# Routing tables by expert on 32 partitions, rows without empty ones, modulation units inside the router

## The reference, cut to what matters

```python
g_idx = argmax(h @ grp_w + grp_b)                 # one group of 4
top_v, top_i = top_k(e_logit_of_that_group, 2)    # two of its 8 experts
w = g_prob * softmax(top_v)
out[token] += w * ((silu(x @ w_gate[e]) * (x @ w_up[e])) @ w_down[e])   # for both experts e
x = x + g2 * out
```

## Time and profile before

| | |
|---|---|
| three runs | 3595.5 us median (3585.95 to 3603.7) |
| the profiled execution | 3583.24 us, its span 3581.4 us |
| PE / VectorE / ScalarE / POOL busy | 86% / 34% / 21% / 13% |
| granted PE clock, mean | 0.919 |
| chain that ended last, by engine | PE 66%, DMA 18%, VectorE 10% |
| of it waiting for expert weights | 16% |
| read from and written to DRAM | 616.92 MB, 42.99 MB |

### The profile page before, as it was taken

How to read it: one execution, slowest core, us unless ns; L and a number is a source line. 1 busy time by engine, 2 the same in 40 slices (tenths; PEclk the granted TensorE clock), 3 DMA queues, 4 the chain that set the end, 5 groups by cost and what they waited for, 6 DMA issues and landing times.

```text
span 3581.4 us, 36439 instructions
## 1 busy us (share of the span) xinstructions
PE 3069.8 (86%) x15346; PEld 2112.8 (59%) x15346; DVE 1235.5 (34%) x2375; ACT 744.8 (21%) x1331; POOL 472.5 (13%) x477
## 2 busy tenths in 40 slices
PE   5979598888849889869888865999998888899997
PEld 3757555444437655355454425888646677488875
DVE  4984500000035533230000005323273875332334
ACT  3233111000022143201000003212111233222222
POOL 0130122221110033012222210000001321000000
PEclk9989699999978999979999987999998898999998
DMA  6572499999851231259999963222212002122221
GB/s 243 194 181 97 157 358 398 411 397 396 332 203 60 71 122 67 120 184 396 402 394 400 385 257 117 94 94 94 77 60 97 1 1 83 36 94 99 89 86 50
DMA packets 138697, 662.37 MB, mean 185 GB/s; under 512 B 9504, under 2 KB 81568, under 8 KB 104608
## 3 DMA queue, kind: packets, MB, share of 16 engines
q0 software_dynamic: 40560, 428.89, 31.3%
q1 hardware_dynamic: 96816, 226.09, 17.7%
q10 hardware_dynamic: 1152, 4.98, 0.4%
HBM read 616.92 MB, written 42.99 MB: 184 GB/s over the span
## 4 chain that ended last, share of the span: by engine, by line
PE 66%; DMA 18%; DVE 10%; ACT 2%; issue 2%; POOL 1%; POOLq 1%; DVEq 0%; SPq 0%; ACTq 0%
PE ps L87 64%; DMA ring<-in_exp_up,wix 16%; DVE scr L101 3%; PE ps L90 2%; DVE scr L109 1%; ACT hT L93 1%; DVE hT L109 1%; DVE scr L115 1%; DVE scr L121 1%; DVE hT_r L101 1%; DVE scr L112 1%; POOLq L134 1%; DVE ring_r L101 1%; ACT scr L93 1%; POOL ring L130 1%
## 5 line engine op out<-in xcount | busy, mean ns | idle before, releaser
L87 PE MATMUL ps<-ring,scr 128*64 128x512 f32 (+3 forms) x3136 | 757.8, 577 | 115.5 <-DMA ring<-in_exp_up,wix 114.1
L87 PE MATMUL ps<-ring_r 128*128 128x512 f32 (+1 forms) x2544 | 754.1, 378 | 37.2 <-DVE hT_r L101 36.6
L87 PEld LDWEIGHTS ps<-ring,scr 128*64 128x64 f32 (+2 forms) x3136 | 305.1, 160 | 482.5 <-issue 472.2
L87 PEld LDWEIGHTS ps<-ring_r 128*128 128x128 f32 x2544 | 471.8, 192 | 149.5 <-issue 47.2
L87 PE MATMUL ps<-scr,ring 128*128 128x128 f32 (+2 forms) x3744 | 481.9, 292 | 56.2 <-DMA ring<-yrows,nix 30.9
L87 PEld LDWEIGHTS ps<-scr,ring 128*128 128x128 f32 x3744 | 450.6, 200 | 85.2 <-issue 34.8
L87 PE MATMUL ps<-hT_r,ring_r 128*128 128x512 f32 (+1 forms) x1224 | 462.8, 378 | 0.0
L101 DVE TENSOR_TENSOR scr<-scr,ps 64x512 f32<-64x512 f32 (+1 forms) x72 | 49.7, 691 | 844.8 <-ACT scr L93 525.7
L87 PE MATMUL ps<-scr_r,ring_r 128*128 128x512 f32 x1104 | 259.6, 395 | 0.6 <-DVE scr_r L101 0.6
L87 PEld LDWEIGHTS ps<-hT_r,ring_r 128*128 128x128 f32 x1224 | 236.2, 193 | 40.1 <-issue 1.8
L87 PE MATMUL ps<-ring 128*128 128x512 f32 (+9 forms) x712 | 201.8, 520 | 47.4 <-ACT ring L97 24.9
(11 more groups left out here) (143 smaller groups left out, 2548.7 us busy)
## 6 DMA issues: line engine op xcount, KB each, us to landing
ring<-in_ffn_w SPq DMA_DIRECT2D x66, 1024.0 KB, 5.3
ring<-in_mod_w SPq DMA_DIRECT2D x16, 2048.0 KB, 7.7
ring<-in_mod_w SPq DMA_DIRECT2D x16, 1024.0 KB, 4.9
yrows<-scr SPq DMA_DIRECT2D x88, 128.0 KB, 9.3
yrows<-scr SPq DMA_DIRECT2D x20, 512.0 KB, 11.2
ring<-in_exp_gate SPq DMA_DIRECT2D x4, 2048.0 KB, 14.8
ring<-in_exp_up SPq DMA_DIRECT2D x4, 2048.0 KB, 19.2
ring<-in_exp_down SPq DMA_DIRECT2D x4, 2048.0 KB, 23.6
```

The lines of the kernel that those rows point to most:

```text
L87: return self.real.matmul(o, l, r, start=start, stop=stop) if self.real else Quiet()
```

## The change

- **Counts and tables by expert.** The router's weights are padded to 64 columns, and even and odd kt use different halves of the PE columns; the two halves are summed in the matmul that turns the logits (`half_sum`). The counts come out with experts on 32 partitions; rank, place, capacity and overflow of each expert are then one column, and one matmul (`r_p`) spreads 160 columns of results over all partitions. The ranks of the tokens are one bank (`r_k`). One-hot matrices are built in four instructions in all. Work that only the combine needs (`w1`, `w2`, `ox`) stands at the end.
- **Rows.** `rt` holds token numbers above the bound for empty slots, and the gather has `bounds_check`, which leaves those rows out. `yrows` has 1536 rows, one per token and choice, and POOL scatters each block's results straight to them (`pool_outputs`), again without the empty slots. The combine reads them with plain loads on SP. The zero writes are gone.
- **Ends.** No stage end stands between blocks and branch; only POOL reports (`"further"`) to SP.
- **Modulation.** The four units of layer 0's mixture are loaded in halves into scratch and multiplied between the router's steps.
- **Splits.** The first two parts of "at" and "ffn1" are made by ScalarE in the combine and by POOL (`POOL_LOWER`).

```diff
-        for b in range(32):
-            hst = M.hst[:, (b % 2) * 1024:(b % 2) * 1024 + 1024]
-            e.wait_ge(*ps.emptied("e_d", l, b, 0))
...
-                    e.dma(yrows[128 * b:128 * b + 64, 512 * q:512 * q + 512], hst[64 * q:64 * q + 64, 0:512]).then_inc(
-                        *y_out[b % 2].up(l, b, by=16))
-        if l == 0:
-            e.wait_ge(*yg_in[512].of(0))
-            for u in M.mod.units:
-                weights_load(e, 3 + u % 3, ("mod", 1, u), I["mod_w"][1, u], 8, 512)
+        e.wait_ge(*y_out[0].of(l, 30))
+        e.wait_ge(*y_out[1].of(l, 31))
+        e.wait_ge(*pool_step.of("further", l))
+        for a, n in chunks(M.T):
+            for i in tiles_of(a, n):
+                for q in range(2):
+                    r = 768 * q + 128 * i
+                    e.dma(moe_y(l, i, q), yrows[r:r + 128, :]).then_inc(*y_in[a].up(l, i, q, by=16))
...
+        mod_load(0)
+        fixed(0, 0)
+        mod_load(1)
+        fixed(0, 1)
+        mod_load(2)
+        fixed(0, 2)
+        mod_load(3)
+        fixed(1, 0, 1, 2)
...
+    def pool_outputs(e, l, b, *signal):
+        M = moes[l]
+        y = M.hst[:, (b % 2) * 1024:(b % 2) * 1024 + 1024]
+        e.wait_ge(*ps.emptied("e_d", l, b, 0))
+        if wide(b):
+            e.wait_ge(*ps.emptied("e_d", l, b, 1))
+            e.scatter(yrows, M.rw[:, b:b + 1], y, bounds_check=1535, oob_is_err=False).then_inc(*signal)
+        else:
+            e.scatter(yrows.rearrange("r (h c) -> (r h) c", h=2), M.rn[:, b:b + 1], y[:, 0:512], bounds_check=3071,
+                      oob_is_err=False).then_inc(*signal)
...
         for b in range(32):
             if b + 3 < 32:
                 fetch_x(b + 3)
             fetch(b + 2, 0, 1)
             if b >= 1:
                 fetch(b + 1, 2)
-        e.wait_ge(*y_out[0].of(l, 30))
-        e.wait_ge(*y_out[1].of(l, 31))
+                store(b - 1)
+        store(31)
...
-        T3 = M.xr[0].rearrange("p (a b) -> p a b", a=32)
-        go(e.tt(T3, row(M.key), col(M.key), ALU.is_ge))
-        go(e.reduce(M.rank, T3, ADD))
+        go(e.ts(cmp, key, kc, ALU.is_ge))
+        go(e.reduce(rank, cmp, ADD))
...
         pool_blocks(e, l)
-        stage_end(e, f"ov{l}", "act", "dve", "pe")
-        e.wait_ge(*dve_step.of(l, "ox"))
-        e.overflow(nix[0:1, 40:41], lambda: pool_further(e, l), *own_signals)
+        e.drain()
+        e.overflow(nix[0:1, 16:17], lambda: pool_further(e, l), *own_signals)
+        e.drain().then_inc(*pool_step.up("further", l))
...
-        for b in range(47):
-            if b not in WIDE:
-                a = 64 if b < 32 else 0
-                e.dma(yrows[128 * b + a:128 * b + 128, :].rearrange("p (k c) -> p k c", c=128), zero[a:128]).then_inc(
```

More of the change, by code:

```diff
@@ L965, in rows @@
                 m.then_inc(*ps.fill("r_h", l, i, q))
-        for i in range(NT // 2):
-            rows(i)
+        if l == 0:
+            pe_mod_pieces(e, 1)
+        rows(0)
+        rows(1)
         e.wait_ge(*dve_step.of(l, "aa"))
-        for i in range(NT):
-            o = ps.take("r_k", l, i)
-            e.wait_ge(*ps.ready("r_k", l, i))
-            for j in range(i):
-                e.matmul(o[:, 0:32], k("ones"), M.AA[:, j, :], j == 0, False)
-            e.matmul(o[:, 0:32], k("tri"), M.AA[:, i, :], i == 0, True).then_inc(*ps.fill("r_k", l, i))
@@ L975, in pe_router @@
         o = ps.take("r_n", l)
         e.wait_ge(*ps.ready("r_n", l))
-        for j in range(NT):
-            m = e.matmul(o[:, 0:32], k("ones"), M.AA[:, j, :], j == 0, j == NT - 1)
-        m.then_inc(*ps.fill("r_n", l))
-        for i in range(NT // 2, NT):
-            rows(i)
+        e.matmul(o[0:32, 0:32 * NT], k("ones")[:, 0:32], M.AA, True, True).then_inc(*ps.fill("r_n", l))
+        o = ps.take("r_k", l)
+        e.wait_ge(*ps.ready("r_k", l))
+        for s in range(1, NT):
+            e.matmul(o[:, 32 * s:32 * NT], k("ones"), M.AA[:, 0:32 * (NT - s)], s == 1, False)
@@ new lines, in pe_router @@
+        e.matmul(o[:, 32:32 * NT], k("tri"), M.AA[:, 32:32 * NT], False, True)
+        e.matmul(o[:, 0:32], k("tri"), M.AA[:, 0:32], True, True).then_inc(*ps.fill("r_k", l))
+        if l == 0:
+            pe_mod_turn(e, M.mod, 0)
+            pe_mod_pieces(e, 2)
+        o = ps.take("r_p", l)
+        e.wait_ge(*ps.ready("r_p", l))
+        e.wait_ge(*dve_step.of(l, "by_expert"))
+        e.matmul(o[:, 0:160], k("ones")[0:32, :], M.rows[0:32, :], True, True).then_inc(*ps.fill("r_p", l))
+        rows(2)
@@ L990, in act_router @@
+        m.then_inc(*ps.fill("r_r", l))
+        for i in range(4, NT):
+            rows(i)
+        if l == 0:
+            pe_mod_turn(e, M.mod, 2)
+            pe_mod_turn(e, M.mod, 3)
     def act_router(e, l):
@@ new lines, in dve_router @@
+        cnt, key, cmp, kc, rank, place, cap, cc, oc, ov, o6, rows = (p32(x) for x in (
+            M.cnt, M.key, M.cmp, M.kc, M.rank, M.place, M.cap, M.cc, M.oc, M.ov, M.o6, M.rows))
+        e.wait_ge(*ps.filled("r_n", l))
+        e.reduce(cnt, ps.ap("r_n", l)[0:32, 0:32 * NT].rearrange("p (t e) -> p e t", e=32), ADD).then_inc(*ps.empty("r_n", l))
+        e.wait_ge(*ps.emptied("r_n", l))
+        go(e.stt(key, cnt, 32.0, p32(k("krow")), MUL, ADD))
+        go(e.ttr(cmp, key, id32, scale=1.0, scalar=0.0, op0=MUL, op1=ADD, accum_out=kc))
@@ L1916, in pool_attention @@
     def pool_attention(e):
+        for j in range(2):
+            part_lower(e, ("at", j))
         for n in range(32):
```

422 lines of the change are left out of this document (230 added, 192 removed).

## The result

The changed kernel takes 3447.1 us (median of 4 runs, 3444.5 to 3450.2) against 3593.9 before (4 runs, 3586.0 to 3603.7): a ratio of 0.959, 95% interval 0.957 to 0.962, **faster by 147 us**. The forecast was 3499, the range 3463 to 3536: right in sign, outside the range. I account for the 133.

What follows compares the result with a forecast made beforehand. Blocks 9 to 31 were taken as DMA-bound, earlier ones PE-bound, routers bound by small steps. Terms 24 + 24 + 22 + 6 + 18.5 + 2 - 0.3 = 96 off 3583.2 give 3487, 3499 us on the median's footing; range 3463 to 3536.

Steps and rivals of the forecast that it cites:

- 3, rows: Block loops: leaving empty slots out of gather and write in blocks 9 to 31 saves 22 us, bounds 0 and 44.
- rows save in full: Rival for the later blocks: all bytes of empty slots are saved, 44 us, ending at 3477; chance 0.2.
- the engine swizzle: Later blocks: each DMA engine serves eight fixed partitions, engine 0 keeps nearly its whole load, rows save about 8 us.
- rows save nothing: Rival for the later blocks: first partitions' engines keep their load or empty slots still make transfers; 3521, chance 0.2.
- 1, router of layer 0: Layer 0's router: shorter logits, choice, ranks and tables put `rt` 32.5 us earlier; 8.5 given back, 24 us saved.
- 2, router of layer 1: Layer 1's router: the same with four tiles and no modulation, 26 less 2 given back, 24 us saved.
- 4, scatter on POOL: Block loops: 32 scatter issues per layer, about 0.95 us plus 0.3 each, are covered by POOL's wait; cost 0.
- the rival that ends slower: Rival for the block loops: scatters hold up POOL's queue and delay later fetches, 3665 at 9 us each; chance 0.03.
- 5, fetch of y: End of the blocks: scatter, unwaited drain and plain loads save 4 and 8 us; 6 us taken, bounds 12 and -14.
- the rival that charged it: Rival for the blocks' end: the second drain costs as much as the first, 10.10 us, giving 3519; chance 0.1.
- 6, after the combine: Layer 0 after the combine: 25.3 us shrink to 6.8, POOL's splits hidden by the norm; 18.5 us saved.
- 7, splits of ffn1: Layer 1 before ffn1: 4.49 us of VectorE leave the chain, some splitting enters ScalarE; 2 us saved.

Runs made afterwards that it cites:

- gather_all_halves: Changed kernel, but every empty slot gathers row 767 and narrow blocks' x rows come as 2 KB half rows onto all 128 partitions; 3431.0 us.
- before_skip_x: Kernel before, with only the x gathers leaving empty slots out, all y rows still written by SP; 3526.8 us, ratio 0.982.
- late_fixed: Changed kernel, last row tiles ahead of the table matmuls, two modulation units behind, block 1's weights held until the first x gather landed; 3434.0 us.
- splits_dve: Changed kernel, with the subtractions for the attention's and ffn1's first two weights moved from POOL back to VectorE; 3440.9 us.
- gather_all: Changed kernel, but every empty slot gathers row 767, while the scatter still leaves empty slots out; 3509.7 us.

## Why the prediction was right or wrong

- **3, rows: wrong, and the largest part of the miss.** Forecast 22, bounds 0 and 44; it was 69. The step that failed is "At 396 and 395 GB/s that is 18.7 and 25.2 us, 44 in all; that is the upper bound". It took the rate for a property of the chip. The rate was what x rows on half of the partitions left of it (the later blocks run at 395 to 400 GB/s in the kernel before and at 425 to 426 in gather_all_halves, at the same DMA share of 1.01): the gathers alone gave 53, the writes' move to POOL's queue 21 (priced at nothing), and scattered bytes cost nothing in the loops. The rival "rows save in full" had the right direction and the same wrong bound. The 8 us that the engine swizzle led to, and the rival that rows save nothing, are refuted by before_skip_x.
- **1, router of layer 0: half.** Logits (22.7 us from the norm's start, now 19.6) and choice (10.3, now 6.3) saved the 3 and 4 of the forecast. Ranks and tables were to save 26.5 and saved 17.4 (372.66 to 416.4 before, 368.33 to 394.7 now): the step that failed is "So `rt` stands 32.5 earlier, at 384". VectorE was done with the tables at 384.8, but I let the table matmuls start at once, and PE was in a modulation unit that waited for weights until 388.35. Then "the twelve matmuls (1.1)" took 5.3: before, most of them ran beside VectorE's steps, now all twelve follow the last of these. They took 5.3 us at a granted clock of 0.50 (the 1.2 GHz level), and 2.8 in late_fixed at 1.00. The give-back behind it, 8.5 in the forecast, was 10.8 (from `rt` to x 5.1 us before, 15.9 now). In late_fixed `rt` comes at 382.6 and x at 398.4, where the forecast had 384 and 398: the lost time ahead of `rt` is order and clock. The give-back is not: from `rt` to x late_fixed still takes 15.8, since the last row write is issued behind `rt` (384.4) and the gather 9.4 later.
- **2, router of layer 1: right**, 21.8 for 24.
- **4, scatter on POOL: right.** A scatter took 1.01 us on the mean of 64, hidden; the rival that ends slower did not come about.
- **5, fetch of y: wrong by 18.** The step that failed is "drain 10.1 without waiting for the landing": it was 4, which makes 12. The other 6 are a margin: the forecast's own parts gave 4 and 8, and it took 6 in case the drain should grow. The second drain was to cost nothing, rightly; the rival that charged it is out.
- **6, after the combine: right but for one row.** 13.7 for 18.5. "The splits move to POOL, 4.60 each, hidden by the norm (9 us)": the first was not beside the norm but beside VectorE's sums, where a step of 0.41 took 4.24.
- **7, splits of ffn1: wrong sign**, -4 for +2, by the same hold-up; splits_dve gives 3 of each back.
- **The footing.** 12.3 us were added for the median of before; the changed kernel's profile was no such distance below its own, so 15 more went missing. The upper end of the range, 3536, is 3 above what its terms add up to (3499 + 22 + 12).

## What to carry to other kernels

A DMA share of 1.00 says that the engines are busy, not that bytes set the pace (here it stood beside 385 and beside 425 GB/s): look at how long one packet of the main stream takes beside other traffic, and at which partitions that traffic goes to. A transfer onto 64 partitions can hold up a stream over 128 by more than its bytes; spreading it over all partitions gave more here than leaving out half of its rows (79 us against 63, both counted from gather_all). When a chain is shortened, ask of each queue what now stands just ahead of its last link: a load that is not urgent yet, or a matmul that waits for one.

## What the runs showed of the hardware

- Gathering the 2118 empty slots of the later blocks as 4 KB rows, those of narrow blocks onto the lower 64 partitions, cost 2.4 times their bytes (53 us); with the narrow blocks' rows as two half rows over 128 partitions, gathering the empty slots costs 6 us in both loops (1035.0 against 1028.9), less than its bytes.
- Rows written from SBUF to DRAM beside the weights cost nothing in the loops (1058.4 against 1058.9 us), if issued from POOL's queue; the same writes from SP's cost 21 us.
- A weight packet of 16 KB takes 617 to 627 ns undisturbed. In the kernel before it takes 780 beside rows that go to partitions 0 to 63, 614 beside rows that go to all 128, and 619 beside a write.
- POOL's drain took 10.1 to 10.2, 5.1 or 3.5 us with everything landed; its cause is open.
- A VectorE step of 0.41 us took 4.24 beside a subtraction on POOL of 4.51; a reciprocal of 128x6 beside one took its usual 0.19.
